# A hybrid decoder trunk: both token mixers reordered (paired slabs, all convolution taps off TensorE, projections by column units)

## The reference

```python
def hybrid_mixer(h, ...):
    proj = h @ w_in                                  # 1024 x 3584
    a, b, p, gc, gp = jnp.split(proj, IN_SPLITS, axis=-1)   # 512, 512, 512, 1024, 1024 columns
    yc = conformer_conv(a, b, ...)    # u = a * sigmoid(b); causal depthwise convolution, 31 taps,
                                      # 512 channels; layer norm; silu; @ w_conv_out (512 x 1024)
    yp = multiscale_pool(p, ...)      # window means 2, 4, 8, 16 minus p; @ w_pool; * pool_scale
    merged = jax.nn.sigmoid(gc) * yc + jax.nn.sigmoid(gp) * yp
    return merged @ w_out                            # 1024 x 1024

for layer in range(DEPTH):
    h = rms_norm(x, mix_norm[layer])
    x = x + hybrid_mixer(h, ...)
    h = rms_norm(x, ffn_norm[layer])
    x = x + (swiglu(h, ...) if layer % 2 == 0 else moe_ffn(h, ...))
return rms_norm(x, final_norm)
```

## Time and profile before

| | |
|---|---|
| median of 3 runs | 1507.9 us (1507.87 to 1508.37) |
| the profiled execution | 1507.77 us |
| its span | 1506.0 us |
| TensorE's mean granted clock | 0.991 of full speed |
| busy: PE, DVE, ACT, POOL | 1458.6, 1193.4, 993.0, 152.0 us |
| bytes read from HBM | 432.73 MB |

### The profile page before, as it was taken

The page is one execution under the profiler, slowest core; times in us unless marked ns, Lnnn a source line. Parts: engine busy times, 40 slices in busy tenths (PEclk is TensorE's granted clock), DMA queues, the critical chain, the costliest instruction groups (busy, mean ns, idle before and its releaser), DMA issues.

```text
span 1506.0 us, 18439 instructions
## 1 busy us (share of the span) xinstructions
PE 1458.6 (97%) x6617; PEld 1200.0 (80%) x6617; DVE 1193.4 (79%) x979; ACT 993.0 (66%) x880; POOL 152.0 (10%) x236
## 2 busy tenths in 40 slices
PE   7989999999989899999999999999999999999997
PEld 5877888888867688888888888878888888888885
DVE  4767554455867798998899899899889889889986
ACT  5665534435764577767777777776777777777764
POOL 6860400000760000000000000000000000000000
PEclk9999999999999799999999999999999999999999
DMA  9445555555336489999899899998988989999890
GB/s 351 158 139 181 184 182 195 189 175 193 123 117 238 173 324 394 345 341 379 339 357 365 335 364 356 356 385 328 385 346 338 383 333 365 357 356 382 332 369 29
DMA packets 186224, 434.42 MB, mean 288 GB/s; under 512 B 7825, under 2 KB 11201, under 8 KB 186177
## 3 DMA queue, kind: packets, MB, share of 16 engines
q1 hardware_dynamic: 184704, 432.20, 77.1%
q10 hardware_dynamic: 1472, 1.61, 0.3%
HBM read 432.73 MB, written 1.05 MB: 288 GB/s over the span
## 4 chain that ended last, share of the span: by engine, by line
PE 81%; POOL 6%; DVE 4%; issue 4%; ACT 3%; DMA 0%; POOLq 0%; SPq 0%; DVEq 0%; ACTq 0%
PE bank L1108 25%; PE bank L1110 25%; PE bank L1109 25%; POOL work L450 4%; PE bank L1257 2%; ACT w_hi L511 2%; DVE w_lo L765 2%; POOL gates L406 1%; DVE dT_lo L1032 1%; PE bank L1328 1%; PE bank L1353 1%; POOL mix L423 1%; PE bank L1354 0%; DVE xs L892 0%; PE bank L1336 0%
## 5 line engine op out<-in xcount | busy, mean ns | idle before, releaser
L765 DVE TENSOR_TENSOR w_lo<-raw,w_hi 128x2048 fp32r<-128x2048 f32 x315 | 716.9, 2286 | 241.6 <-ACT w_hi L511 240.7
L511 ACT ACTIVATE w_hi<-raw 128x2048 fp32r<-128x2048 f32 x315 | 602.5, 1918 | 361.2 <-PE bank L1110 354.3
L1108 PE MATMUL bank<-w_hi,dT_hi 128*128 128x512 f32 (+1 forms) x912 | 360.7, 395 | 8.2 <-DVE w_lo L765 3.7
L1110 PE MATMUL bank<-w_hi,dT_lo 128*128 128x512 f32 (+1 forms) x912 | 355.0, 389 | 0.0
L1109 PE MATMUL bank<-w_lo,dT_hi 128*128 128x512 f32 (+1 forms) x912 | 354.6, 389 | 0.0
L1108 PE MATMUL bank<-w_hi,cT_hi 128*128 128x512 f32 x568 | 223.4, 393 | 0.0
L1110 PE MATMUL bank<-w_hi,cT_lo 128*128 128x512 f32 x568 | 221.3, 390 | 0.0
L1109 PE MATMUL bank<-w_lo,cT_hi 128*128 128x512 f32 x568 | 221.1, 389 | 0.0
L1108 PEld LDWEIGHTS bank<-w_hi,dT_hi 128*128 128x128 f32 x912 | 172.0, 189 | 47.9 <-issue 6.6
L1110 PEld LDWEIGHTS bank<-w_hi,dT_lo 128*128 128x128 f32 x912 | 171.8, 188 | 36.2
L1109 PEld LDWEIGHTS bank<-w_lo,dT_hi 128*128 128x128 f32 x912 | 172.0, 189 | 33.5
(11 more groups left out here) (189 smaller groups left out, 1282.9 us busy)
## 6 DMA issues: line engine op xcount, KB each, us to landing
raw<-in_moe_w_gate_dram SPq DMA_DIRECT2D x96, 1024.0 KB, 7.0
raw<-in_moe_w_up_dram SPq DMA_DIRECT2D x72, 1024.0 KB, 8.7
raw<-in_moe_w_down_dram SPq DMA_DIRECT2D x72, 1024.0 KB, 7.3
raw<-in_w_in_dram SPq DMA_DIRECT2D x28, 1024.0 KB, 5.3
mix<-in_moe_w_up_dram SPq DMA_DIRECT2D x16, 1024.0 KB, 8.8
gates<-in_moe_w_down_dram SPq DMA_DIRECT2D x16, 1024.0 KB, 9.4
gates<-in_moe_w_up_dram SPq DMA_DIRECT2D x16, 1024.0 KB, 9.0
work<-in_moe_w_down_dram SPq DMA_DIRECT2D x16, 1024.0 KB, 9.3
```

Of the source, the lines that this page charges most:

```text
L511: act.activation(w_hi[:, u % SPLIT, 0:width], place[slot][:, 0:width], ACT.Copy).then_inc(hi_ready, 1)
L765: dve.tensor_tensor(w_lo[:, u % SPLIT, 0:width], place[slot][:, 0:width], w_hi[:, u % SPLIT, 0:width].bitcast(F32), ALU.subtract).then_inc ...
L1108: nc.tensor.matmul(dst, a_hi, b_hi, start=start, stop=False)
L1110: return nc.tensor.matmul(dst, a_lo, b_hi, start=False, stop=stop)
```

## The change

It touches both mixers, the borders between stages and the last units of the dense stage. The expert loop stays, except for bank arguments.

1. **Paired slabs.** The first two slabs of a mixer hold 256 columns of b and the same 256 of a each (`paired_units`, each unit from two transfers), so that the first slab gives u for chunks 0 and 1, the second for 2 and 3. u is transposed in two halves, amid units U+2 and U+4. Then come three gate slabs, then p (U+10, U+11), then the last gate slab (U+12, U+13).
2. **No taps on PE.** Diagonals and their matmuls are gone. DVE has chunks 0 and 2 whole, with two running sums each (even and odd taps) and one addition at the end; ACT makes the 62 products of chunks 1 and 3, chunk by chunk, and POOL sums them (60 adds).
3. **Statistics between the units of the last gate slab.** Between U+12 and U+13 PE does the mean, the pooling windows and the variance. Centring, squares and normalising go in two halves. ACT applies Silu in one instruction per chunk; DVE makes both the rounded copy and the rest.
4. **Projections by column units.** Units of w_conv_out and w_out, and two of the dense w_down, are 512 rows x 512 columns (`column_unit`), so each result's left half is finished by whole units. Merging, transposing of merged rows (into the tiles `dT`, `cT`) and the residual's addition go half by half, with the left half's transposes amid the last unit.
5. **`normed_input`** is the common start of a stage: add the left half to x, split up to unit U+1, operand's left half, add right half, split U+2, sum of squares, operand's right half (transposed amid the first unit).
6. PSUM banks are passed on from stage to stage (`MixerBanks`, `DenseBanks`).

```diff
-    TP, TV = 16, 19
-    PRODUCTS = sorted([(j, CC - 1, j) for j in range(TAPS)] + [(2 * (j - TV) + 1, CC - 2, j) for j in range(TV, TAPS)])
-    PRODUCTS = [(c, j) for _, c, j in PRODUCTS]
+    DVE_CHUNKS, ACT_CHUNKS = (0, 2), (1, 3)
+    PRODUCTS = [(c, j) for c in ACT_CHUNKS for j in range(TAPS)]
...
+    def column_unit(w, k, c):
+        return (4, N, lambda: k_rows(w)[:, k:k + 4, c:c + N])
+    def paired_units(w, c, d):
+        part = lambda j, c: k_rows(w)[:, 4 * j:4 * j + 4, c:c + N // 2]
+        return [(4, N, (lambda j=j: part(j, c), lambda j=j: part(j, d))) for j in range(2)]
     def mixer_units(l):
-        columns = (CD, 0, 2 * CD) + tuple(3 * CD + N * j for j in range(4))
-        units = [u for c in columns for u in slab_units(w_in[l], c)]
+        units = paired_units(w, CD, 0) + paired_units(w, CD + N // 2, N // 2)
+        for c in (GATES, GATES + N, GATES + 2 * N, 2 * CD, GATES + 3 * N):
+            units += slab_units(w, c)
         units.append((GROUPS, GO, lambda: w_pool[l].rearrange("g c o -> c g o")))
-        return units + row_units(w_conv_out[l], 0, CC) + row_units(w_out[l], 0, KD)
+        units += [column_unit(w_conv_out[l], 0, c) for c in (0, N)]
+        return units + [column_unit(w_out[l], k, c) for k in (0, 4) for c in (0, N)]
...
-            pool.wait_ge(taps_ready, L)
-            tap_diagonals(0)
-            inverse_root()
...
+            def normed_input(U, gain, banks, x_whole):
+                split_to(U + 2)
+                operand(0, hT_of, gain, banks)
+                split_to(U + 3)
+                x_whole()
+                sum_of_squares(0)
+                operand(1, hT_of, gain, banks)
+                sum_of_squares(1)
+                split_to(U + 4)
...
-                split_to(U + 2 if l else 1)
-                operand(V_MIX + KD * l, X_BANKS)
+                normed_input(U, V_MIX + KD * l, M.x, x_added if l else x_loaded)
...
+                act.wait_ge(rstd_ready, seen.next(rstd_ready))
+                sigmoid_of_b(0, M.low)
                 split_to(U + 5)
+                u_columns(0)
+                tap_products(l, 7)
...
+                split_to(U + 6)
+                tap_products(l, 9)
+                sigmoid_of_b(1, M.high)
+                split_to(U + 7)
+                u_columns(1)
+                tap_products(l, 11)
+                split_to(U + 8)
+                tap_products(l, 17)
+                gate_half(U + 6, 0, M.low)
                 split_to(U + 9)
+                tap_products(l, 21)
+                split_to(U + 10)
+                tap_products(l, 28)
+                gate_half(U + 8, 1, M.high)
+                split_to(U + 11)
+                tap_products(l, 32)
+                split_to(U + 12)
+                tap_products(l, 39)
+                gate_half(U + 10, 2, M.low)
+                split_to(U + 13)
+                tap_products(l, 43)
+                split_to(U + 14)
+                tap_products(l, 50)
...
+                tap_products(l, 56)
                 split_to(U + 15)
+                tap_products(l, len(PRODUCTS))
+                split_to(U + 16)
...
+                gated_pool(0)
+                split_to(U + 17)
+                gated_pool(1)
+                split_to(U + 18)
+                merge(0)
+                split_to(U + 19)
+                operand(0, mT_hi, mT_lo, None, M.merged)
+                merge(1)
+                split_to(U + 20)
+                operand(1, mT_hi, mT_lo, None, M.merged)
...
+                slab(U, hT_hi, hT_lo, low, fresh=hT_ready, amid=x_right)
+                slab(U + 2, hT_hi, hT_lo, high, amid=lambda: transpose_u(0, M.u))
+                slab(U + 4, hT_hi, hT_lo, low, amid=lambda: transpose_u(1, M.u))
                 slab(U + 6, hT_hi, hT_lo, high)
+                pe.wait_ge(gates_ready, seen.next(gates_ready, TB))
                 slab(U + 8, hT_hi, hT_lo, low)
                 pe.wait_ge(gates_ready, seen.next(gates_ready, TB))
                 slab(U + 10, hT_hi, hT_lo, high)
+                def statistics():
+                    for c in range(CC):
+                        if c in ACT_CHUNKS:
+                            pe.wait_ge(prod_added, len(ADDS) * l + last_add[c])
+                        else:
+                            pe.wait_ge(conv_step, CONV_STEPS * l + (TAPS + 1) * (c // 2 + 1))
...
+                    last.then_inc(mean_done, 1)
+                    pool_windows(M.pooled)
...
+                slab(U + 12, hT_hi, hT_lo, low, between=statistics)
```

More of the change, by code:

```diff
@@ L516, in rstd, with sum_of_squares, operand @@
                 return small[:, 6 + b:7 + b]
-            def sums_of_squares():
-                for b in range(TB):
-                    act.activation(junk, xs[:, b, :], ACT.Square, accum_out=small[:, b:b + 1]).then_inc(sumsq_ready, 1)
-                    act.wait_ge(sumsq_ready, seen.next(sumsq_ready))
-            def operand(gain, banks):
-                for k in range(KD):
+            def sum_of_squares(b):
+                act.activation(junk, xs[:, b, :], ACT.Square, accum_out=small[:, b:b + 1]).then_inc(sumsq_ready, 1)
+                act.wait_ge(sumsq_ready, seen.next(sumsq_ready))
+            def operand(h, dst, gain, banks):
+                for k in range(4 * h, 4 * h + 4):
                     if k % 2 == 0:
@@ new lines, in mixer @@
+                act.wait_ge(unit_used, seen.at(unit_used, U + 12))
+                for b in range(TB):
+                    act.activation(tokP[:, b, :], bank[M.high[b]][:, :], ACT.Copy, scale=rstd(b)).then_inc(p_ready, 1)
+                tap_products(l, 56)
+                split_to(U + 15)
+                tap_products(l, len(PRODUCTS))
+                split_to(U + 16)
+                for i in range(2):
+                    act.wait_ge(centred, seen.next(centred))
+                    act.activation(sq[:, 2 * i * S:2 * (i + 1) * S], work[:, 0, 2 * i * S:2 * (i + 1) * S],
+                                   ACT.Square).then_inc(centred_sq, 1)
@@ L616, in mixer @@
+                split_to(U + 17)
+                gate_half(U + 14, 3, M.low)
                 split_to(U + 19)
-                operand(None, MERGED_BANKS)
+                operand(0, mT_hi, None, M.merged)
+                split_to(U + 20)
+                operand(1, mT_hi, None, M.merged)
                 split_to(U + 21)
@@ new lines, in add_to_x, with all_of, normed_input @@
+            def add_to_x(h, banks, finished):
+                finished()
+                for b in range(TB):
+                    part = xs[:, b, h * N:(h + 1) * N]
+                    dve.tensor_tensor(part, bank[banks[h][b]][:, :], part, ALU.add).then_inc(x_ready, 1)
+            def all_of(unit):
+                return lambda: dve.wait_ge(unit_used, seen.at(unit_used, unit))
+            def normed_input(U, gain, banks, x_left, x_right):
+                x_left()
+                split_to(U + 2)
+                operand(0, hT_of, hT_rest, gain, banks)
+                x_right()
@@ L1129, in slab, with rows @@
                         between()
-            def rows(U, units, a_hi, a_lo, blocks, first_bank, start, stop, fresh=None, between=None, by_halves=False):
+            def rows(U, units, a_hi, a_lo, dst, start, stop, between=None):
                 for j in range(units):
@@ L1152, in rows, with column_rows, transpose_half @@
                         between()
-            def transpose_x(source, banks, waits):
-                for k in range(KD):
-                    if k % 4 == 0:
-                        waits(k // 4)
+            def column_rows(U, k0, a_hi, a_lo, dst, start, stop, fresh=None, amid=None, after=6):
+                pe.wait_ge(lo_ready, seen.at(lo_ready, U + 1))
+                s = U % SPLIT
+                steps = [(b, kk) for b in range(TB) for kk in range(4)]
+                for n, (b, kk) in enumerate(steps):
+                    if fresh is not None and b == 0:
+                        pe.wait_ge(fresh, seen.next(fresh))
+                    if amid is not None and n == after:
+                        amid()
+                    w = slice(kk * N, (kk + 1) * N)
+                    last = product(bank[dst[b]][:, :], a_hi(k0 + kk, b), a_lo(k0 + kk, b), w_hi[:, s, w], w_lo[:, s, w],
+                                   start and kk == 0, stop and kk == 3)
+                last.then_inc(unit_used, 1)
+            def transpose_half(source, banks, h):
+                for k in range(4 * h, 4 * h + 4):
                     for b in range(TB):
@@ L1281, in _ @@
                     pe.wait_ge(silu_ready, seen.at(silu_ready, TB * c))
-                slab(g, hT_hi, hT_lo, low, fresh=hT_ready if c == 0 else None,
-                     between=(lambda: hidden_transposes(TB, 4, 2)) if c else None)
+                slab(g, hT_hi, hT_lo, low, fresh=None if c else hT_ready, amid=None if c else lambda: transpose_x(DENSE.x, 1),
+                     between=(lambda: hidden_transposes(TB, 4, DENSE.high)) if c else None)
```

534 lines of the change are left out of this document (275 added, 259 removed).

## The result

The changed kernel takes 1527.95 us (median of four runs, 1527.51 to 1528.74), the kernel before 1507.88 us (four runs, 1507.16 to 1508.37): a ratio of 1.0134, 95% interval 1.0117 to 1.0152. It is 20.1 us slower. The forecast was 1517.8 us with a range of 1508 to 1526: the sign is right, the size is half of what happened, and the time lies above the range. The profiled execution took 1527.51 us with a span of 1525.9 us, 19.9 us more than the span before.

A forecast was written before the change was run, and what follows sets the result against it. TensorE, busy 97% of the span, was taken as the bound. Start +4.9, mixer 0 +1.6, dense -0.5, mixer 1 +2.8 and router +1.1 gave +9.9 on 1507.9, so 1517.8 us, range 1508 to 1526.

The forecast's parts named there:

- POOL's chain: Both mixers: 60 adds, 0.87 us apart when chained, end at T0 + 89.0; PE waits about 15 us at the mean.
- The splits: DVE's weight splits in POOL's window: each costs POOL about 2.05 us beyond the add; nine plus a half-width one, 19.5 us.
- Rival 1: Mixers: POOL is ready in time, stalls and clock loss go, each layer about 17.5 us shorter, 1483 us; chance 0.12.
- rival 3: Mixers: ACT's splits behind products starve PE, or the tail is uncovered, 5 us more per layer, 1528 us; chance 0.10.
- Rival 2: Mixers: a wash, splits overlap POOL's empty stretches or clock stays up; 1505 us, 1511 with one; chance 0.10.
- The reason given for the block: Mixers: DVE's split reads two SBUF tensors, so it locks the shared port and blocks POOL's add for a whole instruction.
- the start: Ahead of mixer 0's first slab matmul: ACT splits units 0 and 1 before the first operand, PE starts at 20.0, +4.9 us.
- the router's product: After mixer 1: right add, right transposes, copies and the product's second half come in a row, +1.1 us.
- The merge's wait: Layer tail: DVE's pool gating, two splits and left merge in a row end about 2.2 us late; new waits +2.5 us.
- The last dense unit's order, the late tile and one more table load lie under matmuls: 0: End of the dense stage: these changes are covered by matmuls and cost nothing; the stage was put at -0.5 us.
- the routing at 0: Routing stage: no added time in the sum; SP's later wait for spare places is covered by matmuls and the routing.
- the clock: Behind the 15 us stall at the mean: pooling windows and part of the variance at half speed, +2.5 us per layer.

The follow-up runs named there:

- Experiments 1 to 3: Changed kernel with 16 chunk 3 taps on DVE: 1503.07 us; with 60 adds in two sums per chunk: 1518.67 us; with 8 chunk 3 taps on DVE: 1517.77 us.
- the shared taps alone: Changed kernel with DVE taking the last 16 of the 31 taps of chunk 3 from ACT and POOL, 44 adds per layer: 1503.07 us.
- all five edits: Changed kernel with 16 taps moved to DVE and splits or gate work reordered at start, dense tail, routing and merge: 1483.16 us.
- experiment 4: Changed kernel with ten DVE weight splits per mixer reading one SBUF tensor instead of two, output wrong: 1516.21 us.
- Experiment 6: Changed kernel with the last dense slab's gate work on ACT and DVE ahead of the split of unit U+32: 1525.45 us.
- experiment 8: Changed kernel with DVE splitting its half of the second expert unit before the router's second operand, not after the routing: 1525.26 us.
- Experiment 9: Changed kernel with the left half merged one gating and one split earlier on DVE: 1521.06 us.
- experiment 5: Changed kernel with 60 matmuls that nothing reads filling PE's wait at the mean in both mixers: 1525.01 us.
- experiment 3: Changed kernel with DVE taking the last 8 of the 31 taps of chunk 3, so POOL has 52 adds per layer: 1517.77 us.

## Why the prediction was right in sign and wrong in size

**Right: POOL's chain.** Spacing (0.87 us forecast, 0.88 found) and end (T0 + 89.0 forecast, T0 + 92.0 in mixer 0 with its cold start, T0 + 89.7 in mixer 1) hold, and so does the wait ("about 15 us", found 15.6 and 15.3). Experiments 1 to 3 show it: sixteen adds fewer take 12.9 us off the wait, the wait goes with the number of adds, and unchaining them takes 6 us off. That the end was met so closely is in part luck. The first add ended 1.2 us later than forecast. The splits were put at 19.5 us, nine and a half of them at 2.05; in mixer 1 eight adds of 2.4 to 2.9 us and three of 1.3 to 1.5 stand for some 17 us beyond adds of 0.75. Waits for ACT's products were put at 0.5 us and are 2.8. Rival 1 (POOL ready in time, 1483 us) was not what this kernel does, and its price was too high: with the shared taps alone 24.9 of the 35 us came back. Of the rest, 5.2 us stand as a wait for DVE, and the 2.5 us of clock per layer did not come back. That all five edits give 1483.16 is chance, since four of them are no part of that rival. Chance too is that rival 3 was priced at 1528: its queues did not starve PE (in neither mixer does PE wait for a weight split), and the layer's tail is 0.6 us longer than forecast, and POOL's end 0.7 us later, not 5 us together. Rival 2's "1511 with one of the two" does not follow from its own terms, which give 1507 with the splits alone and 1515 with the clock alone. The reason given for the block was too narrow, as experiment 4 shows; the price did not depend on it.

**Right: the start** (+4.9 against +5.3), **the router's product** (+1.1 against +1.3) and the expert loop. The merge's wait was priced within the layer's tail (2.5 us for new waits), and is 2.2 us long.

**Wrong: "The last dense unit's order, the late tile and one more table load lie under matmuls: 0".** This is the step that failed most: the dense stage was put at -0.5 and took +3.3, an error of 3.8 us. A unit of matmuls does lie there, but both ACT and DVE split the next unit ahead of the last gate, so PE stands 2.07 us, and the clock's fall behind it costs 1.7. Experiment 6 takes both away, 3.8 us by the rows, though the median fell by only 2.5.

**Wrong: the routing at 0.** The sum went through SP's and POOL's queues there and not through DVE's. The expert units' splits are done one unit later than before, which leaves 2 x 2.24 us in a row ahead of the first expert operand where there was one, and PE's wait for it is 3.4 us, not 1.2. The stage took 2.9 us more; experiment 8 gives back 2.7.

**Wrong in size: the clock.** The sum had one slow stretch per layer, behind the stall at the mean, at 2.5 us; that stretch costs 1.7, since PE is idle through most of it. It had none behind the 2.2 us stall for merged rows, which costs 1.7 us in each mixer of the changed kernel. Experiment 9, which removes the stall, gives 6.9 us where the stall itself is 4.5. With POOL 0.7 us later and a tail of 54.3 us against 53.7 (from POOL's last add to the end of the last slab matmul), mixer 1 is 1.3 us longer than forecast, and mixer 0 likewise.

Together: 0.4 at the start, 1.3 and 1.5 in the mixers with the router, 3.8 in dense, 2.9 in the routing, 9.9 us of the 10 by which the span was missed. The range failed for the same reason: its high end took in bounds of the terms that were priced, and nothing for the places put at 0, the largest of which were worth 3.8 and 2.9.

**Left open.** The taps of chunk 2 were not put back on PE, so their 6.9 us per layer are read from the count of records and not from a run; nor were the other gains of the change (paired slabs, projections by column units) run alone. And why a stall of 2.2 us has a slow stretch behind it in one kernel and none in another (experiment 5), and why runs of one kernel lie in two groups (experiment 3), no experiment here explains.

## What to carry to other kernels

When work leaves the busiest engine, lay out the chain of the engine that gets it add by add, against the time at which the other one comes for it: here POOL's sums were 15 us late, and giving sixteen of them to an engine with room turned 20 us of loss into 5 us of gain. A new order has to be followed at every border through every in-order queue: a weight split one place too early on ACT or DVE cost 2 to 5 us at the start, the merge, the dense tail and the routing, and moving each by one place brought it back. A place that is put at nothing should have its queue written out, or be given a bound in the range.

## What the runs showed of the hardware

- An add on POOL that needs the result of the one just before starts 0.87 to 0.88 us after it at 128x256 fp32, while adds of two sums in turn start 0.70 us apart. Of the 10 us that 60 such adds save, 6 came back in each mixer; the rest went into waits for ACT's products.
- A POOL add that meets DVE's weight split ends 0.6 us after the split does, whether DVE reads two SBUF tensors (2.29 us) or one (1.23 us), and splits that began while an add was under way took up to 2.6 to 2.7 us.
- Short stalls of PE, 2.0 to 2.6 us, often had stretches at the lower clock of 3.4 to 10 us at or behind them in which PE was busy nearly throughout (1.7 us of time for 3.4 us), but not always: in experiment 5 three of five had none. The stall of 15.6 us had a longer one, 13.7 us, that cost no more, 1.7 us, since PE was idle for most of it.
